# Another queue for the turned stores, loads by pair of heads, and another order of the heads

## The chip, the core and the metric

The kernel is one program on one core of a Trainium2 chip. Its metric is the device time of one execution in microseconds (us). TensorE multiplies, VectorE and ScalarE do the element-wise work, GpSimd helps, and the transfers (DMAs) are issued by SyncE (SP), ScalarE and GpSimd and carried out by 16 DMA engines. SP and ScalarE issue to a hardware queue each, GpSimd to a software queue.

## The reference

One step of an encoder layer, for a prompt of 1024 rows and for 8 sequences of 16 new rows each with 256 cached ones (the sample). Width 1024, 16 heads of 64 in four groups of four.

```
xn = rmsnorm(x, g_attn)
aq, ak, av, bq, bk, bv, cq, ck, cv, dq, dk, dv, df = split(xn @ w_in)   # w_in: 1024 x 2820
A: stick-breaking attention     w = exp(log_sigmoid(z) + later sum of -softplus(z)), causal
B: window of 128 and chunks of 64, 2 key/value heads for 4 query heads, sinks, T5 bias
C: differential attention       softmax(s1) - lam * softmax(s2), T5 bias; then rmsnorm of the head
D: forgetting attention         softmax(s + F_q - F_k), causal; F = cumsum(log_sigmoid(df + b_f))
h = x + concat(A, B, C, D) @ w_out
h = h + square(relu(rmsnorm(h) @ w_up)) @ w_down                        # 1024 x 4096
h = h + sigmoid(h @ w_ple_gate) * (p @ w_ple_proj);  y = rmsnorm(h)
```

The outputs are y, the new keys and values of each group, and the log gates. All is float32.

## The kernel before

The 1152 rows (1024 of the prompt and 128 of the sample) make nine tiles of 128, the ninth being the sample. A float32 product is made of rounded parts, a high one and a low one: `three` issues three matmuls (high x high, high x low, low x high).

**Projection.** First come the values of A and B with the gates (nine units, one for each tile), then the turned operands: queries and keys computed transposed, 128 columns of `w_in` by 384 rows a unit. `QK` lists 45 such units: for A, C and D the pieces k, q, k, q of three units each, for B k, q, q. A unit is 24 matmuls of 384 columns into one of three PSUM banks. ScalarE writes the high part (`stage_hi`, L443 or L449, and for keys a float32 copy, L448), VectorE the low part (`stage_lo`, L510, L512), and both parts are stored to scratch tensors in HBM (`q2`, `k2`: "q_turned_A" and so on). There are two staging buffers by `m % 2`: ScalarE waits for the store of unit m - 2 (`st_q`) before it writes unit m. Between the units TensorE transposes blocks of the key caches and of the new keys (`TURNS`, L638, 46 banks). A bank of the cache goes the same way: high part on ScalarE (L435), low part on VectorE (L497), into one of two `chl` buffers, stored to `kc2` ("k_cache_turned_A"); ScalarE waits for `st_c` before it overwrites one. For A, C and D each piece of keys has two banks of cache in each of its first two units. A bank of new keys goes to `krow` and from there to the key outputs. ScalarE also splits the next block's weights, one slot a unit (`split`). Last come the values of C and D (nine units) with some small work on gates and biases.

A scratch tensor holds, for each head, 64 rows (C: 32) of one half of the operand's features and then the other part's, so that a matmul over 128 partitions sums high and low. The rows are put there by this view, for all of these stores:

```python
def parts(dst, g, part):
    return dst.rearrange("(x u d) c -> u x d c", u=2, d=HALF[g])[part]
```

With a destination of 256 rows this is 2 x 64 rows for A, B and D (HALF is 64) and 4 x 32 for C. A store of a unit is 128 rows of 1536 bytes (196,608 bytes; two a unit, 90 in all: A 24, B 18, C 24, D 24). One of a cache bank is 128 rows of 2048 bytes (262,144; two a bank, 52 in all: A, C and D 16 each, B 4). GpSimd issues all of them in `qk_out` and `turned_out`, in the order of the units.

**Attention.** A loop runs twice (`heads_loop`). Each pass goes through eight jobs, two heads of each group, in the order AABBCCDD. A job is nine tiles of queries: eight of the prompt, with 128 to 1024 keys (B: up to 256), and the sample. The engines are one or two tiles apart: in step s TensorE does `scores(s + 1)`, `turn_tile(s - 1)`, `values(s - 2)`; ScalarE `evacuate_tile(s - 2)`, `exponentials(s)`; VectorE `maximum(s)`, `out(s - 3)`. VectorE prepares the next job's bias or gates at its seventh tile (`bias(nxt)`, `sample_gates(nxt)`) and waits there for all loads of that job (`job_loaded`). For a head of C, VectorE, ScalarE and GpSimd norm the outputs together in `norm`, at the tiles 5 and 6 of the next job, and GpSimd's last two operations of it (L988, L990) follow ScalarE's n_rstd.

SP issues the loads of a job when the job two before it is done (`o_full`), into one of two buffers: keys (L917), queries (L918), queries with the parts crossed (L921), the sample's cached keys (L923), its new keys (L924), its queries spread out by sequence (L925, and crossed L928), values (L929) and cached values (L930), and then what B, C or D need besides (L934 to L945; the last of B and C is L939). L924, L925 and L928 write pieces of 64 bytes. TensorE's `scores` of a job's first tile waits for all of them.

**The rest.** Output projection, MLP, input embedding and the final norm. These aren't touched.

## Time and profile before

| | |
|---|---|
| Median of 3 runs | 2264.15 us (2262.93 to 2274.48) |
| The profiled execution's own time | 2268.79 us |
| Its span, first to last instruction | 2267.2 us |
| Mean granted clock of TensorE | 0.867 |
| Busy: TensorE, VectorE, ScalarE, GpSimd | 84%, 38%, 28%, 8% of the span |
| Bytes moved by DMA | 196.88 MB, mean 87 GB/s |

The profile is of one execution. A busy share is an average over stages with different limits, so it's read by stretch. The granted clock is a share of full speed (1.00 is 2.4 GHz, 0.50 is 1.2 GHz). A DMA share is the mean busy share of the 16 DMA engines. In a list of waits the thing behind the arrow is what came last by the profile.

### The profile page before, as it was taken

Reading aid. Unit: us, or ns where it says so; the run is one execution under the profiler, and the core shown is the slowest. Engines: PE = TensorE matmul, PEld = TensorE weight load, DVE = VectorE, ACT = ScalarE, POOL = GpSimd, SP = SyncE. Lnnn points to the kernel's source line nnn. Section 1 sums busy time; section 2 is a strip of 40 time slices with the busy share of each in tenths; the row PEclk is TensorE's granted clock in tenths of the full one; section 3 lists DMA queues with packets and bytes.
Section 4 is the critical chain, followed back from the end, with each engine's and each line's share of the span. In section 5 each row is a group of like instructions: output and inputs, shape, how many; then the busy total and the mean of one; then the engine's idle time right before and its main releaser. Section 6 shows DMA issues by size and latency. Waiting matters only on the chain. (4 is left out here: it accounts for less than half of the span.)

```text
span 2267.2 us, 28303 instructions
## 1 busy us (share of the span) xinstructions
PE 1896.3 (84%) x10134; PEld 1710.8 (75%) x10134; DVE 851.6 (38%) x1619; ACT 645.1 (28%) x1387; POOL 188.0 (8%) x272
## 2 busy tenths in 40 slices
PE   6857766775848877668779999999999999999898
PEld 6857666654747776657668889899989989998686
DVE  5211222125525636535543543333333333333334
ACT  5211111014423435423332322122212212221226
POOL 0233233300000100000101000000000000000000
PEclk9978888796667776757769999999999999999999
DMA  5555565515353443544425111111211111120202
GB/s 185 143 121 135 138 149 131 105 62 126 93 130 83 127 108 88 124 116 106 109 63 176 61 56 38 38 38 38 66 47 38 38 38 38 38 65 28 76 18 98
DMA packets 257174, 196.88 MB, mean 87 GB/s; under 512 B 178044, under 2 KB 210624, under 8 KB 257016
## 3 DMA queue, kind: packets, MB, share of 16 engines
q1 hardware_dynamic: 178312, 132.75, 21.2%
q0 software_dynamic: 60032, 57.53, 10.5%
q10 hardware_dynamic: 18688, 4.72, 0.9%
q8 instruction: 88, 1.44, 0.3%
q14 instruction: 54, 0.44, 0.1%
HBM read 144.29 MB, written 54.81 MB: 88 GB/s over the span
## 5 line engine op out<-in xcount | busy, mean ns | idle before, releaser
L1346 PE MATMUL outs<-v_rows,probs_turned 128*128 128x64 f32 x984 | 166.1, 325 | 112.2 <-DVE head_out L1208 84.1
L111 PE MATMUL up<-xt_hi,w_hi_even 128*128 128x384 f32 x768 | 258.0, 336 | 1.8 <-PEq L1399 1.8
L113 PE MATMUL up<-xt_hi,w_lo_even 128*128 128x384 f32 x768 | 257.8, 336 | 0.0
L112 PE MATMUL up<-xt_lo,w_hi_even 128*128 128x384 f32 x768 | 257.6, 335 | 0.0
L1346 PEld LDWEIGHTS outs<-v_rows,probs_turned 128*128 128x128 f32 x984 | 159.0, 244 | 124.8 <-DVE head_out L1208 62.1
L113 PE MATMUL down<-w_hi_odd_b,hidden_lo 128*128 128x512 f32 x576 | 224.5, 390 | 0.0
L112 PE MATMUL down<-w_lo_odd_b,hidden_hi 128*128 128x512 f32 x576 | 224.5, 390 | 0.0
L111 PE MATMUL down<-w_hi_odd_b,hidden_hi 128*128 128x512 f32 x576 | 224.0, 389 | 0.0
L1606 DVE TENSOR_TENSOR h_rows<-down,h_rows 128x1024 f32<-128x1024 f32 x72 | 88.2, 1225 | 236.4 <-PE down L113 236.4
L1571 ACT ACTIVATE hidden_rows<-up 128x384 f32<-128x384 f32 x96 | 47.3, 492 | 417.1 <-PE up L113 417.1
L1314 PE MATMUL scores<-k_turned,q_turned_straight 128*128 128x512 f32 (+5 forms) x224 | 89.9, 519 | 69.5 <-ACT probs L1038 31.1
L111 PEld LDWEIGHTS up<-xt_hi,w_hi_even 128*128 128x128 f32 x768 | 145.0, 189 | 3.2 <-DVE xt_lo L138 2.2
L112 PEld LDWEIGHTS up<-xt_lo,w_hi_even 128*128 128x128 f32 x768 | 145.0, 189 | 0.8
L113 PEld LDWEIGHTS up<-xt_hi,w_lo_even 128*128 128x128 f32 x768 | 144.8, 189 | 0.0
L1599 DVE TENSOR_TENSOR hidden_rows<-hidden_rows 128x384 f32<-128x384 f32 x96 | 53.6, 558 | 223.8 <-ACT hidden_rows L1571 223.8
L113 PEld LDWEIGHTS down<-w_hi_odd_b,hidden_lo 128*128 128x128 f32 x576 | 108.1, 188 | 22.5
L112 PEld LDWEIGHTS down<-w_lo_odd_b,hidden_hi 128*128 128x128 f32 x576 | 108.1, 188 | 22.0
L111 PEld LDWEIGHTS down<-w_hi_odd_b,hidden_hi 128*128 128x128 f32 x576 | 108.2, 188 | 21.9
L888 ACT COPY probs_turned<-turns 128x512 f32<-128x512 f32 (+3 forms) x156 | 68.6, 459 | 148.9 <-PE turns L1333 148.5
L1333 PE MATMUL turns<-cst,probs 128*128 128x128 f32 x520 | 105.7, 333 | 1.7 <-ACT probs L1024 1.7
L1314 PEld LDWEIGHTS scores<-k_turned,q_turned_straight 128*128 128x128 f32 (+1 forms) x224 | 45.9, 260 | 80.8 <-issue 35.8
L1155 DVE TENSOR_REDUCE stats<-scores 128x1 f32<-128x272 f32 (+8 forms) x76 | 51.5, 705 | 79.0 <-PE scores L1318 78.5
(271 smaller groups left out, 3712.5 us busy)
## 6 DMA issues: line engine op xcount, KB each, us to landing
w_raw<-w_up SPq DMA_DIRECT2D x64, 256.0 KB, 2.9
w_raw<-w_down SPq DMA_DIRECT2D x64, 256.0 KB, 3.1
w_raw<-w_in SPq DMA_DIRECT2D x24, 256.0 KB, 7.6
v_rows<-value_rows SPq DMA_DIRECT2D x16, 288.0 KB, 3.7
head_rows<-head_out ACTq DMA_DIRECT2D x16, 288.0 KB, 6.4
head_rows_in<-head_rows POOLq DMA_DIRECT2D x9, 512.0 KB, 4.7
x_rows<-x_prompt SPq DMA_DIRECT2D x8, 512.0 KB, 3.7
k_cache_turned_A<-k_cache_parts POOLq DMA_DIRECT2D x16, 256.0 KB, 12.6
```

The source lines that it names most:

```text
L111: nc.tensor.matmul(out, xh, wh, start=first, stop=False)
L112: nc.tensor.matmul(out, xh, wl, start=False, stop=False)
L113: return nc.tensor.matmul(out, xl, wh, start=False, stop=last)
L888: copy(pt[i % 2][:, b * P:b * P + k], TB[n % 3][:, 0:k]).then_inc(q[f"read{n % 3}"], 1)
L1155: nc.vector.tensor_reduce(st_[:, col:col + 1], src[:, 0:n], AX.X, ALU.max, negate=True).then_inc(q["m_ready"], 1)
L1314: nc.tensor.matmul(S[UNIT[(i, m)] % 2][:, c:c + w], qt[part][own, e, P * t:P * (t + 1)], kt[own, e, k0 + c:k0 + c + w], start=part == 0, s ...
L1333: last = nc.tensor.transpose(TB[n % 3][:, (y - b) * P:(y - b + 1) * P], block_src, ident)
L1346: last = nc.tensor.matmul(dst, w[:, y * P:(y + 1) * P], vr[:, e, first_block(i) + y, :], start=y == 0, stop=y == nb - 1)
L1571: nc.scalar.activation(R[:, f % 2, :], U[f][:, 0:GT], ACT.Relu).then_inc(relu_d, 1)
L1599: nc.vector.tensor_tensor(R[:, f % 2, :], R[:, f % 2, :], R[:, f % 2, :], ALU.mult).then_inc(sq_d, 1)
L1606: nc.vector.tensor_tensor(H[:, t, :], DN[t % 2][:, :], H[:, t, :], ALU.add).then_inc(dn_add, 1)
```

## The change

The stores of turned operands and of turned cache are issued by ScalarE, to its hardware queue, in the same order and with the same views: those of unit m - 1 at the top of unit m's turn. GpSimd keeps the key rows and the values. In attention the order of the jobs is ABABCDCD, and buffers go by the job's number instead of by the head. Values are loaded once for the pair of heads of a group, in rows twice as wide, with semaphores of their own (`v_in0`, `v_in1`), for which only `values` waits. Keys and queries are loaded with the sample's columns, and GpSimd makes the sample's operands of them in `spread_operands`, three copies of 128 x 128 in the place of the DMAs L924, L925 and L928; TensorE waits for them before the sample's scores. `softplus` gets a wait for the weight buffer where a job of A follows another group.

```diff
-        def turned_out(x):
-            m, u = TURN_LIST[x]
-            if u[0] == "k":
...
-            else:
-                g, y = CACHE_LOADS[u[1]]
+        def k_rows_out(x):
+            _, u = TURN_LIST[x]
+            f = u[1]
+            if u[0] == "k" and x + 1 == k_turned(f):
+                _, g, _, pair, _, _ = QK[f * NG]
                 pool.wait_ge(c_read, x + 1)
-                dst = kc2[g][2 * P * u[2]:2 * P * u[2] + 2 * P, 512 * y:512 * y + 512]
-                n = caches_before(x) % CR
-                for part in range(2):
-                    nc.gpsimd.dma_start(parts(dst, g, part), chl[:, n, part, :].bitcast(F32)).then_inc(st_c[n], 16)
-        def qk_out(m):
-            _, g, kind, pair, _, n = QK[m]
-            pool.wait_ge(qk_lo, m + 1)
-            dst = (k2 if kind == "k" else q2)[g][2 * P * pair:2 * P * pair + 2 * P, GT * n:GT * n + GT]
-            for part, src in enumerate((stage_hi(m), stage_lo(m))):
-                nc.gpsimd.dma_start(parts(dst, g, part), src.bitcast(F32)).then_inc(st_q[m % 2], 16)
+                own = slice(P * pair, P * pair + P)
...
         for t in range(TILES):
             values_out(t, t, 0, 384)
-        x = 0
-        for m in range(len(QK)):
-            qk_out(m)
-            for _ in TURNS[m]:
-                turned_out(x)
-                x += 1
+        for x in range(NTURN):
+            k_rows_out(x)
...
+        def cache_out(x):
+            _, u = TURN_LIST[x]
+            if u[0] == "c":
+                g, y = CACHE_LOADS[u[1]]
+                act.wait_ge(c_read, x + 1)
+                dst = kc2[g][2 * P * u[2]:2 * P * u[2] + 2 * P, 512 * y:512 * y + 512]
+                n = caches_before(x) % CR
+                for part in range(2):
+                    act.dma_start(parts(dst, g, part), chl[:, n, part, :].bitcast(F32)).then_inc(st_c[n], 16)
...
+        def qk_out(m):
+            _, g, kind, pair, _, n = QK[m]
+            act.wait_ge(qk_lo, m + 1)
+            dst = (k2 if kind == "k" else q2)[g][2 * P * pair:2 * P * pair + 2 * P, GT * n:GT * n + GT]
+            for part, src in enumerate((stage_hi(m), stage_lo(m))):
+                act.dma_start(parts(dst, g, part), src.bitcast(F32)).then_inc(st_q[m % 2], 16)
...
         x = 0
         for m, (blk, g, kind, pair, col, n) in enumerate(QK):
+            if m:
+                qk_out(m - 1)
+                for y in range(x - len(TURNS[m - 1]), x):
+                    cache_out(y)
...
+        qk_out(len(QK) - 1)
+        for y in range(NTURN - len(TURNS[len(QK) - 1]), NTURN):
+            cache_out(y)
...
-vr, vc = sb("v_rows", [P, 2, TILES, HD]), sb("v_cache_rows", [P, 2, 16, HD])
...
-qt = [sb(f"q_turned_{n}", [P, 2, SEQ], F32R) for n in ("straight", "crossed")]
-kt = sb("k_turned", [P, 2, SEQ], F32R)
+vr, vc = sb("v_rows", [P, 2, TILES, P]), sb("v_cache_rows", [P, 2, 16, P])
...
+qt = [sb(f"q_turned_{n}", [P, 2, TILES * P], F32R) for n in ("straight", "crossed")]
+kt = sb("k_turned", [P, 2, TILES * P], F32R)
...
-JOBS = [(g, e) for g in GROUPS for e in range(2)]
+JOBS = [(g, e) for pair in ("AB", "CD") for e in range(2) for g in pair]
...
 def odd(i):
-    return JOBS[i // TILES][1]
+    return i // TILES % 2
+def value_buf(i):
+    return GROUPS.index(group(i)) % 2
...
-                done = q[f"job_in{e}"]
+                done = q[f"job_in{x}"]
                 half = HALF[g]
                 own = q2[g][bass.ds(P * h, P), :]
                 keys_ = k2[g][bass.ds(P * kvh, P), :]
-                crossed = [(slice(x, x + half), slice(y, y + half)) for z in range(0, P, 2 * half) for x, y in ((z, z + half), (z + half, z))]
-                def by_sequence(ap):
-                    return ap.rearrange("p (b n) -> p b n", b=DEC_B)
-                def spread(part, e):
-                    return by_sequence(qz[part][:, e, :].bitcast(F32))[:, :, 0:DEC_S]
                 sp.wait_ge(q["o_full"], at("o_full", TILES * (job - 1)))
...
-                sp.dma_start(kt[:, e, :].bitcast(F32), keys_[:, 0:SEQ]).then_inc(done, 16)
-                sp.dma_start(qt[0][:, e, :].bitcast(F32), own[:, 0:SEQ]).then_inc(done, 16)
-                for to, of in crossed:
-                    src = q2[g][bass.ds(P * h + of.start, half), :]
-                    sp.dma_start(qt[1][to, e, :].bitcast(F32), src[:, 0:SEQ]).then_inc(done, 16)
+                sp.dma_start(kt[:, x, :].bitcast(F32), keys_).then_inc(done, 16)
+                sp.dma_start(qt[0][:, x, :].bitcast(F32), own).then_inc(done, 16)
+                for y in range(0, P, 2 * half):
+                    for to, of in ((y, y + half), (y + half, y)):
+                        sp.dma_start(qt[1][to:to + half, x, :].bitcast(F32), q2[g][bass.ds(P * h + of, half), :]).then_inc(done, 16)
                 n = P * cached(g)
-                sp.dma_start(ks[:, e, :, 0:n].bitcast(F32), by_sequence(kc2[g][bass.ds(P * kvh, P), :])).then_inc(done, 16)
-                sp.dma_start(ks[:, e, :, n:n + DEC_S].bitcast(F32), by_sequence(keys_[:, SEQ:SEQ + P])).then_inc(done, 16)
-                sp.dma_start(spread(0, e), by_sequence(own[:, SEQ:SEQ + P])).then_inc(done, 16)
-                for to, of in crossed:
-                    src = q2[g][bass.ds(P * h + of.start, half), :]
-                    sp.dma_start(spread(1, e)[to], by_sequence(src[:, SEQ:SEQ + P])).then_inc(done, 16)
-                sp.dma_start(vr[:, e, :, :], vrows[:, bass.ds(V_COL[g] + HD * kvh, HD)].rearrange("(t p) d -> p t d", p=P)).then_inc(done, 16)
-                sp.dma_start(vc[:, e, 0:nb, :], cache[:, bass.ds(vcol + HD * kvh, HD)].rearrange("(s p) d -> p s d", p=P)).then_inc(done, 16)
+                sp.dma_start(ks[:, x, :, 0:n].bitcast(F32), kc2[g][bass.ds(P * kvh, P), :].rearrange("p (b n) -> p b n", b=DEC_B)).then_inc(done, 16)
+                if e == 0:
+                    v, nb = GROUPS.index(g) % 2, DEC_B * cached(g)
+                    w = HD if g == "B" else P
+                    cache = i[f"cache_{g.lower()}_kv"]
+                    vcol = 128 if g == "B" else 256
+                    sp.wait_ge(q["o_full"], at("o_full", TILES * (job_of(GROUPS[GROUPS.index(g) - 2], 1) + 1) - (0 if g in "CD" else NT)))
+                    sp.dma_start(vr[:, v, :, 0:w], vrows[:, bass.ds(V_COL[g] + w * j, w)].rearrange("(t p) d -> p t d", p=P)).then_inc(q[f"v_in{v}"], 16)
+                    sp.dma_start(vc[:, v, 0:nb, 0:w], cache[:, bass.ds(vcol + w * j, w)].rearrange("(s p) d -> p s d", p=P)).then_inc(q[f"v_in{v}"], 16)
                 if g in "BC":
                     hb = h + (4 if g == "C" else 0)
                     src = toep[bass.ds(hb, 1), 127:127 + P * (BAND - 1)].rearrange("o (p c) -> (o p) c", p=P)
-                    sp.dma_start(bi[:, e, :], src[:, 0:2 * P]).then_inc(done, 16)
+                    sp.dma_start(bi[:, x, :], src[:, 0:2 * P]).then_inc(done, 16)
                     src = toep[bass.ds(hb, 1), 127:127 + DEC_S * (BAND - 1)].rearrange("o (p c) -> (o p) c", p=DEC_S)
                     for b in range(DEC_B):
-                        sp.dma_start(bs[b * DEC_S:(b + 1) * DEC_S, e, 0:P + DEC_S], src[:, 0:P + DEC_S]).then_inc(done, 16)
+                        sp.dma_start(bs[b * DEC_S:(b + 1) * DEC_S, x, 0:P + DEC_S], src[:, 0:P + DEC_S]).then_inc(done, 16)
...
+                    sp.dma_start(fq[:, x, :], fcum_q[bass.ds(h, 1), :, :].rearrange("o p t -> (o p) t")).then_inc(done, 16)
...
+        def spread_operands(job):
+            e, n = job % 2, P * cached(JOBS[job][0])
+            job_loaded(pool, job)
+            pool.sem_inc(pool_passed, 1)
+            def by_sequence(ap):
+                return ap.rearrange("p (b n) -> p b n", b=DEC_B)
+            for part in range(2):
+                nc.gpsimd.tensor_copy(by_sequence(qz[part][:, e, :])[:, :, 0:DEC_S],
+                                      by_sequence(qt[part][:, e, SEQ:SEQ + P])).then_inc(q["spread"], 1)
+            nc.gpsimd.tensor_copy(ks[:, e, :, n:n + DEC_S], by_sequence(kt[:, e, SEQ:SEQ + P])).then_inc(q["spread"], 1)
...
             for job in range(len(JOBS)):
+                spread_operands(job)
                 spread_new(job)
                 if JOBS[job][0] == "C":
...
+            if i >= 2 and group(i - 2) != "A":
+                wait_weights_free(act, i)
             nc.scalar.activation(b, z, ACT.Abs).then_inc(q["a_abs"], 1)
...
+            if is_sample(i):
+                pe.wait_ge(q["spread"], at("spread", 3 * (job + 1)))
...
         def values(i):
-            e, nb, c = odd(i), blocks(i), cached(group(i))
+            e, nb, c = value_buf(i), blocks(i), cached(group(i))
+            own = slice(0, HD) if group(i) == "B" else slice(HD * JOBS[i // TILES][1], HD * JOBS[i // TILES][1] + HD)
             w = pt[i % 2]
             dst = OP[:, HD * (i % 2):HD * (i % 2 + 1)]
             for b in range(0, nb, 4):
                 wait_read(pe, WHERE[("tile", i, b)])
             pe.wait_ge(q["o_read"], at("o_read", i))
+            if i % TILES == 0 and JOBS[i // TILES][1] == 0:
+                pe.wait_ge(q[f"v_in{e}"], at(f"v_in{e}", 64 if group(i) in "CD" else 32))
```

Left out are the renamed indices (`job % 2` for the buffer, `JOBS[job][1]` for the head) and the counts of the semaphores.

## Rows read from the trace of the kernel before

**Rows 1.** Busy time, clock and DMA by stretch: start:end, us, each engine (instructions)

```profile
74.00:441.00 367.00, 246.15 (x1244) 237.04 (x1243) 69.02 (x123) 58.50 (x125) 116.92 (x154) 0.82 0.57 130
441.00:508.00 67.00, 55.79 (x230) 41.51 (x228) 15.04 (x27) 10.73 (x16) 6.91 (x12) 0.88 0.26 80
508.00:1190.00 682.00, 485.75 (x3096) 439.11 (x3096) 334.61 (x808) 267.46 (x656) 35.87 (x51) 0.70 0.44 106
1190.00:2267.00 1077.00, 1052.23 (x5256) 939.82 (x5256) 397.98 (x601) 272.44 (x509) 22.53 (x42) 0.98 0.17 54
```

**Rows 2.** Waits of ScalarE, 74 to 441: us in total, times, longest

```profile
ACT x_rows L443 <- DMA k_turned_A<-x_rows: 36.7, 3, 19.6
ACT k_cache_parts L435 <- DMA k_cache_turned_D<-k_cache_parts: 36.5, 4, 17.0
```

**Rows 3.** Timeline of TensorE: two matmuls with 23 between them

```profile
203.03 0.34 PE L111 MATMUL mm<-xt_hi,w_hi_even 128*128 128x384 f32 x1
...
207.19 0.34 PE L111 MATMUL mm<-xt_hi,w_hi_even 128*128 128x384 f32 x1
```

**Rows 4.** GpSimd's stores by line: L361 (turned), then L330 (values)

```profile
DMA to landing us min/median/max: 3.9/9.7/21.6
...
DMA to landing us min/median/max: 2.1/2.3/9.7
```

**Rows 5.** Busy time by stretch again; the last two columns are DMA share and GB/s

```profile
229.50:231.50 2.00, 2.00 (x14) 2.00 (x13) 0.00 (x0) 0.00 (x0) 0.43 (x1) 1.00 0.26 53
468.20:468.90 0.70, 0.70 (x4) 0.57 (x4) 0.00 (x0) 0.70 (x1) 0.00 (x0) 1.00 0.95 371
1500.00:1600.00 100.00, 100.00 (x510) 91.21 (x509) 34.59 (x50) 20.90 (x40) 0.00 (x0) 1.00 0.14 43
509.00:527.00 18.00, 1.35 (x6) 1.35 (x6) 0.00 (x0) 0.39 (x2) 0.00 (x0) 0.50 1.01 251
826.00:852.00 26.00, 24.67 (x187) 22.98 (x186) 13.29 (x29) 11.99 (x28) 0.46 (x1) 0.86 0.66 153
```

**Rows 6.** Waits of VectorE for loads, 560 to 1200: total, times, longest

```profile
DVE bias_sample L1117 <- DMA head_scalar<-rel_bias: 35.6, 3, 18.8
...
DVE head_scalar_negated L1114 <- DMA head_scalar<-swa_sinks: 28.1, 2, 14.4
DVE bias_sample L1101 <- DMA bias_sample<-fcum_sample: 21.9, 2, 11.5
```

**Rows 7.** Timeline of VectorE: start, us, what, idle before it

```profile
640.88 0.15 DVE L1114 TENSOR_SCALAR head_scalar_negated<-head_scalar 128x1 f32<-128x1 f32 x1 [13.67 <-DMA head_scalar<-swa_sinks]
```

**Rows 8.** Timeline of SP's issues, 615 to 675

```profile
619.84 0.35 SPq L917 DMA_DIRECT2D k_turned<-k_turned_B  x1
...
651.42 0.35 SPq L917 DMA_DIRECT2D k_turned<-k_turned_C  x1
...
656.16 0.70 SPq L924 DMA_DIRECT2D k_sample_turned<-k_turned_C  x1
...
665.31 0.39 SPq L929 DMA_DIRECT2D v_rows<-value_rows  x1
...
672.83 0.36 SPq L939 DMA_DIRECT2D head_scalar<-rel_bias  x1
```

**Rows 9.** Timeline of GpSimd, 725 to 800

```profile
730.54 0.45 POOL L976 TENSOR_TENSOR new_probs_by_seq<-probs,masks 128x128 f32<-128x128 f32 x1 [49.03 <-DVE probs L1180]
...
763.45 1.16 POOL L988 TENSOR_TENSOR head_out<-head_out,stats 128x576 f32<-128x576 f32 x1 [22.72 <-ACT stats L1046]
764.69 1.40 POOL L990 TENSOR_TENSOR head_out<-head_out,diff_gain_rows 128x576 f32<-128x576 f32 x1
766.03 0.69 POOL L999 DMA_DIRECT2D b_kv_sample<-value_rows  x1
```

**Rows 10.** Timeline of ScalarE and TensorE in the second head of D

```profile
838.36 1.04 ACT L1038 ACTIVATE probs<-probs,stats 128x896 f32<-128x896 f32 x1 [0.90 <-DVE stats L1155]
...
839.97 0.37 PE L1305 MATMUL scores<-k_sample_turned,q_sample_spread_straight 128*128 128x272 f32 x1
```

More of the change, by code:

```diff
@@ L726, in encoder @@
             primed_sem = sem("att_primed")
-            pe_passed = sem("pe_passed_a_wait")
+            pe_passed, pool_passed = sem("pe_passed_a_wait"), sem("pool_passed_a_wait")
             NAMES = {
                 "job_in0": "loads of the even head", "job_in1": "loads of the odd head",
-                "turned": "PE: a bank of transposes is full",
+                "turned": "PE: a bank of transposes is full", "v_in0": "loads of the values of a pair of heads of A or C",
+                "v_in1": "the same of B or D", "spread": "GpSimd: the sample's queries and new keys are spread",
                 "read0": "bank 0 is evacuated", "read1": "bank 1", "read2": "bank 2",
@@ L807, in loads, with job_of, of_bias @@
             def loads(g):
-                turned = 13 if g == "C" else 9
-                return turned + {"A": 2, "B": 12, "C": 12, "D": 4 + DEC_B}[g]
-            per = {"job_in0": 16 * sum(map(loads, GROUPS)), "turned": len(ORDER), "s_full": len(UNITS),
+                return (7 if g == "C" else 5) + {"A": 0, "B": 10, "C": 10, "D": 2 + DEC_B}[g]
+            def job_of(g, e):
+                return JOBS.index((g, e))
+            def of_bias(job):
+                return sum(g in "BC" for g, _ in JOBS[:job])
+            per = {"job_in0": 16 * sum(loads(g) for g, _ in JOBS[0::2]), "v_in0": 64, "v_in1": 64, "spread": 3 * len(JOBS), "turned": len(ORDER), "s_full": len(UNITS),
                    "b_max": 2 * TILES, "m_ready": len(UNITS) - 2 * TILES, "e_ready": len(UNITS) - 2 * TILES,
@@ L816, in encoder @@
                    "stored0": 16 * 4, "stored1": 16 * 4}
-            per["job_in1"] = per["job_in0"]
+            per["job_in1"] = 16 * sum(loads(g) for g, _ in JOBS[1::2])
             per.update({f"read{x}": len(range(x, len(ORDER), 3)) for x in range(3)})
@@ L870, in job_loaded @@
             def job_loaded(eng, job):
-                e = JOBS[job][1]
+                e = job % 2
                 eng.wait_ge(q[f"job_in{e}"], at(f"job_in{e}", 16 * sum(loads(JOBS[x][0]) for x in range(e, job + 1, 2))))
@@ L899, in body @@
                             h = 2 * j + e
+                            x = job % 2
                             kvh = j if g == "B" else h
-                            cache = i[f"cache_{g.lower()}_kv"]
-                            nb = DEC_B * cached(g)
-                            vcol = 128 if g == "B" else 256
-                            done = q[f"job_in{e}"]
+                            done = q[f"job_in{x}"]
                             half = HALF[g]
@@ L1048, in store @@
                     def store(j, job):
-                        g, e = JOBS[job]
+                        (g, e), x = JOBS[job], job % 2
                         if g == "C":
@@ L1106, in bias @@
                     def bias(job):
-                        g, e = JOBS[job]
-                        k = job - 2 + 1
+                        g, e = JOBS[job][0], job % 2
+                        k = of_bias(job) + 1
                         job_loaded(dve, job)
@@ L1343, in values @@
                         pe.wait_ge(q["o_read"], at("o_read", i))
+                        if i % TILES == 0 and JOBS[i // TILES][1] == 0:
+                            pe.wait_ge(q[f"v_in{e}"], at(f"v_in{e}", 64 if group(i) in "CD" else 32))
                         if not is_sample(i):
                             for y in range(nb):
-                                last = nc.tensor.matmul(dst, w[:, y * P:(y + 1) * P], vr[:, e, first_block(i) + y, :], start=y == 0, stop=y == nb - 1)
+                                last = nc.tensor.matmul(dst, w[:, y * P:(y + 1) * P], vr[:, e, first_block(i) + y, own], start=y == 0, stop=y == nb - 1)
                             last.then_inc(q["o_full"], 1)
```

50 lines of the change are left out of this document (22 added, 28 removed).

## The prediction

> **What bounds the kernel now.** I read the table by stretch first [rows 1]. The MLP stretch is TensorE alone, at its full clock, with 98% busy; the change doesn't touch it. The stretch of the turned operands (74 to 441 us) and attention (508 to 1190 us) hold 1049 of the 2267 us, with TensorE's granted clock at 0.82 and 0.70, which means that it idles and then runs part of its work at 1.2 instead of 2.4 GHz. Those two are what the change touches.
>
> In the first, ScalarE's waits say what ends last: it may not overwrite `stage_hi` or `chl` before earlier stores have landed [rows 2]. TensorE needs far less than the stretch takes. At the full clock one unit of 24 matmuls takes 207.19 - 203.03 = 4.16 us [rows 3], so 45 units need 187 us; with the 46 banks of transposes (my estimate: 0.5 us each) 210 us. The stretch takes 367. The stores are the bound.
>
> Why are they slow? The same GpSimd queue lands a value store of 128 plain rows (192 or 256 KB) in 2.3 us and a turned store of 192 KB in 9.7 us, medians [rows 4]. So it isn't the queue. It is the shape: `parts(...)` makes the destination 2 x 64 rows for A, B and D, and 4 x 32 for C. With two stores of B under way the core's 16 DMA engines are 26% busy, 4 engines' worth, at 53 GB/s; a plain store of the same 1536-byte rows keeps them 95% busy at 371 GB/s [rows 5]. A turned store of B runs on two DMA engines. GpSimd's queue gets its rate from several such stores side by side on different engines: 57% of 16 engines is 9 [rows 1].
>
> In attention I read VectorE's waits. It stands in `bias` and `sample_gates` for the last load of the next head, 28.1 + 35.6 + 21.9 = 85.6 us in seven waits [rows 6], in each half of the heads for B's second, C's first and D's second head. Its `out` comes behind in its order, so TensorE's `values` stops too.
>
> **Part 1, the stores go to ScalarE.** The diff keeps `parts`, so the stores stay on two DMA engines (C: four). Bytes: A, B and D make 66 stores of 196,608 and 36 of 262,144, 22.4 MB; C makes 24 and 16, 8.9 MB. What no row of before shows is on which DMA engines a run of narrow stores of a hardware queue lands. The two ends:
> - On different ones, as now: the stores run side by side and land in time. Then TensorE sets the pace, 210 us at full clock, some 240 with a clock near 0.9 and hiccups: 127 us gained.
> - All on the same two (C: four): they go one behind the other. One engine moved 371/(0.95 x 16) = 24.4 GB/s in the plain store of such rows, 43/(0.14 x 16) = 19 in the MLP, 53/(0.26 x 16) = 12.7 with narrow stores of GpSimd [rows 5]. At 24.4: 22.4/48.8 + 8.9/97.6 = 459 + 91 = 550 us; at 19: 589 + 117 = 706; at 12.7: 1057.
>
> I take the second end, at 24.4, the row of a hardware queue with the very rows of these stores. These engines also carry their sixteenth of 19 MB of loads and key rows: 1.2 MB each at 24.4, +50. In the six pieces of keys with two units of cache turns ScalarE waits for both `chl` buffers before it can issue the next stores, which leaves the engines empty for some 4 us (copies, subtraction, issues, and the start of a store; an estimate): +25. Sum 625 for 367: **+258 us**. I take this end because everything that the rows show of a narrow store is that its shape picks the number of engines, and a queue that also spreads its successive stores is a second property, seen for GpSimd's alone. ScalarE's own cost is 142 issues of about 0.4 us (SP's for a load, [rows 8]), 57 us, under its waits; VectorE's `qk_lo` is done before ScalarE asks. Behind ScalarE's waits stand `split` and the copies, which is why a late store is felt at once.
>
> On this the Trainium skill speaks against the change. Its page "DMA: Bandwidth & Descriptors", section "Why a DMA increments its semaphore by 16 and not by 1", says that the slowest dimensions of both patterns set how many engines a DMA uses, that hardware queues take always the lowest-numbered ones, and that GpSimd's takes them from a round-robin cursor. By that the sum is the +258 above. With the number of engines the trace agrees [rows 5]; which ones a hardware queue takes, no run here shows yet. The same page ("Issuing engine by pattern") calls the hardware path generally faster, which would give the other end's 240 us.
>
> **Part 2, loads of attention.** C's first head: its loads begin at 651.42, the spread DMAs take SP from 656.16 to 665.31, the last is issued at 672.83 [rows 8]. GpSimd's copies replace 9.1 us of it. VectorE reaches its wait about 5 to 7 us after the load's release (640.88 - 13.67 = 627.2, against A's end at 619.84) [rows 7, 8]. In the order ABABCDCD B1's and D1's loads have a whole job of A or C in between: those waits go. C0 still follows a short B: 12.3 us of issues + 2 to land + some 2.5 for values twice as wide, less 7.4 = 9.5 us stay; C1 follows D: about 2.5. So 85.6 - 2 x 12 = 62 us gained. The first job's loads run with the DMA engines full at 251 GB/s [rows 5]; the values and spreads leave the head of it, 4 us gained (an estimate).
>
> **Part 3, GpSimd on the path.** `spread_operands(job)` stands behind `norm` of the C head before. For D0 and D1, GpSimd can begin `norm`'s second half only after ScalarE's n_rstd, right behind exp(6), the exponentials of the tile of 896 keys: 0.6 (my estimate for two activations of nine columns) + 1.16 + 1.40, + 0.69 for a DMA (D0 only) and 3 copies at up to 0.45 (the row of a 128x128 product) [rows 9]. TensorE wants the sample's scores 0.6 us after exp(6): that ended at 839.4 and they began at 839.97 [rows 10]. Late by 5.0 us (D0) and 4.3 (D1), in a job in which TensorE is busy for 24.67 of 26 us [rows 5]: 18 us lost in four. Copies at nothing: 13; above that cover (A, B, C) they cost nothing, since GpSimd idles. ScalarE's new wait in `softplus` holds two tiles of A1 behind B's last turns, about 1 us each half: 2.
>
> Sum of attention: -62 - 4 + 18 + 2 = **-46 us**.
>
> **Sum.** 2267 + 258 - 46 = 2479 in the span. The profiled execution took 2268.8 for a span of 2267.2 and the median of the runs is 2264.15, 0.2% less; so 2475.
>
> **Rivals.**
> 1. The hardware queue spreads its narrow stores too (or uses all 16 engines). For it: 9 engines' worth is what the present queue reaches with the same shapes. Against it: only the software queue is seen doing so. 2267 - 127 - 46 = 2094, so 2090. The point where it decides: below 367 us for 31.3 MB, that is, three and a half engines busy on average at 24.4 GB/s. This is the other side.
> 2. The stores take on that queue what they take now (latency under the mix of loads stays): 2267 - 46 = 2221, so 2218. For it: the share of small transfers and loads stays.
> 3. Rival 2 without the gain of attention, because the waits for loads move elsewhere: C0's wait grows back to 19 us and the D stalls are 10: 2260. Against it: VectorE's waits name loads alone.
>
> **How the numbers follow.** Forecast 0.62; rival 1 0.24; rival 2 0.11; rival 3 0.03. The forecast's own range: 550 us without additions and 70 gained in attention gives 2380; 706 + 75 and 30 gained gives 2650. The whole range must leave out no more than 2 in 10: of rivals 1 to 3 (0.38) it has to reach down to rival 1's middle; I give 2085 to 2640. A measurement can tell 0.5% (11 us) from nothing. Faster: 0.24 + 0.11 = 0.35; same 0.03; slower 0.62.
>
> **What the profile after would show.** Step 1 right: between the two value stretches some 600 us, the share of the DMA engines near 2/16 plus the loads', landings of k_turned above 10 us on ScalarE's queue, the C part quicker than A and D. Wrong: a stretch of 240 us with TensorE's clock above 0.9. Step 2: no wait of VectorE for `head_scalar` of swa_sinks nor for `bias_sample` of fcum_sample; one of some 10 us for rel_bias. Step 3: TensorE's L1305 of D waiting 4 to 5 us for GpSimd. What would make the forecast wrong is, above all, where the hardware queue puts its stores; next the rate of one engine.

## The result, and the profile after

| | before | after |
|---|---|---|
| Median | 2264.9 us (2262.93 to 2274.48, 4 runs) | 2455.33 us (2447.79 to 2456.24, 4 runs) |
| Span of the profiled execution | 2267.2 us | 2454.7 us |
| Mean granted clock of TensorE | 0.867 | 0.843 |

The ratio is 1.0824, with a 95% interval of 1.0787 to 1.0862: 8% slower. The table by stretch of the kernel after answers to [rows 1]:

```profile
74.00:665.00 591.00, 251.43 (x1241) 240.19 (x1239) 69.67 (x123) 59.30 (x124) 8.78 (x13) 0.70 0.24 80
665.00:734.00 69.00, 56.24 (x230) 41.94 (x230) 15.04 (x28) 11.32 (x17) 6.05 (x11) 0.87 0.23 77
734.00:1367.00 633.00, 476.83 (x3096) 426.17 (x3096) 331.13 (x800) 264.64 (x649) 45.20 (x94) 0.72 0.39 109
1367.00:2454.00 1087.00, 1051.56 (x5256) 939.04 (x5256) 402.74 (x608) 276.86 (x517) 25.30 (x47) 0.98 0.17 56
```

The stretch of turned operands took 591 us for 367, and its clock fell to 0.70. SP's first load of attention stands at 733.62 for 508.08 us, 225.5 later. From there to the copy `out_turned` of the last head, at 1364.94 for 1179.41, attention took 631.3 us for 671.3, 40.0 less. What follows took 2.0 more. Sum: 225.5 - 40.0 + 2.0 = 187.5, the difference of the spans.

The list of DMA queues shows what ScalarE's queue (q10) did in the whole stretch and in those parts of it that belong to groups A, C and D, at 75 to 266, 368 to 478 and 478 to 665 us: packets, MB, and the time of its packets as a share of 16 engines.

```profile
q10 hardware_dynamic: 18099, 30.66, 14.0%
...
q10 hardware_dynamic: 4970, 8.57, 12.0%
...
q10 hardware_dynamic: 5188, 8.78, 22.2%
...
q10 hardware_dynamic: 5043, 8.67, 12.4%
```

12.0% of 16 engines is 1.92 engines: two, 96% full. In C it is 3.55 of four. In A one engine moved 8.57 MB / 191 us / 2 = 22.4 GB/s. So on average no more than two engines had work of this queue in A, though several stores were pending; stores side by side on different pairs of engines would show more. The waits of ScalarE in the stretch, which answer to [rows 2]:

```profile
ACT x_normed L449 <- issue: 224.4, 14, 26.5
ACT x_rows L444 <- issue: 57.5, 7, 10.2
ACT x_rows L444 <- DMA q_turned_B<-x_rows: 28.7, 4, 7.5
ACT k_cache_parts L416 <- DMA k_cache_turned_D<-k_cache_parts: 24.2, 4, 9.7
ACT k_cache_parts L416 <- DMA k_cache_turned_A<-k_cache_parts: 23.9, 4, 9.7
```

Most of the idle time has "issue" as its cause, and the timeline shows what that is:

```profile
208.18 0.59 ACT L416 CAST k_cache_parts<-tp 128x512 fp32r<-128x512 f32 x1 [9.66 <-DMA k_cache_turned_A<-k_cache_parts]
208.29 0.52 ACTq L432 DMA_DIRECT2D k_turned_A<-x_rows  x1
...
208.84 0.53 ACTq L432 DMA_DIRECT2D k_turned_A<-x_rows  x1
209.41 17.17 ACTq L425 DMA_DIRECT2D k_cache_turned_A<-k_cache_parts  x4
226.68 0.48 ACT L449 COPY x_normed<-mm 128x384 f32<-128x384 f32 x1 [17.49 <-issue]
```

Two stores are issued in 0.5 us each. The four behind them hold ScalarE for 17.17 us, inside the issuing instructions. The two rows of "issue" are 282 us, and that is only the idle time that ended with an issue: added up over ScalarE's timeline, the issuing instructions took about 396 of the 591 us, because an issue also stands inside many of the waits that are put down to a DMA. By line, the issues of cache stores (minimum, median, maximum in ns):

```profile
L425 ACTq DMA_DIRECT2D k_cache_turned_A<-k_cache_parts x16: 562/4904/7967, 77.3 to 221.6; - x16
L425 ACTq DMA_DIRECT2D k_cache_turned_C<-k_cache_parts x16: 547/1838/4228, 369.2 to 452.8; - x16
L425 ACTq DMA_DIRECT2D k_cache_turned_D<-k_cache_parts x16: 2504/4624/8310, 485.7 to 628.8; - x16
```

In attention, VectorE's and TensorE's waits; VectorE's row answers to [rows 6]:

```profile
DVE bias_sample L1140 <- DMA head_scalar<-rel_bias: 37.1, 4, 15.4
```

```profile
PE scores L1339 <- DMA k_sample_turned<-k_cache_turned_A: 30.1, 3, 24.7
PE scores L1330 <- POOL k_sample_turned L999: 14.7, 4, 4.2
```

The waits for `swa_sinks` and `fcum_sample` are gone. A wait of TensorE for GpSimd's spread keys is new.

### The profile page after: what moved, and what is told of

Its sections match the earlier page's. It is cut to its first block and busy times, and to the rows that moved or that the text cites. A ratio compares the mean times of both kernels' runs of the same rounds, so it can differ in the third digit from the quotient of the medians.

```text
span 2454.7 us, 28218 instructions
## 1 busy us (share of the span) xinstructions
PE 1892.4 (77%) x10134; PEld 1700.2 (69%) x10134; DVE 853.7 (35%) x1619; ACT 648.0 (26%) x1387; POOL 91.1 (4%) x178
## 5 line engine op out<-in xcount | busy, mean ns | idle before, releaser
L1374 PE MATMUL outs<-v_rows,probs_turned 128*128 128x64 f32 x984 | 154.2, 308 | 66.4 <-DVE head_out L1231 36.0
L1374 PEld LDWEIGHTS outs<-v_rows,probs_turned 128*128 128x128 f32 x984 | 146.6, 227 | 79.7 <-DVE head_out L1231 35.9
L642 PE MATMUL tp<-cst,x_normed 128*128 128x128 f32 x56 | 12.6, 348 | 241.3 <-ACT x_normed L449 239.3
L642 PEld LDWEIGHTS tp<-cst,x_normed 128*128 128x128 f32 x56 | 8.4, 176 | 244.8 <-issue 241.4
L516 DVE TENSOR_TENSOR x_rows<-mm,x_rows 128x384 fp32r<-128x384 f32 x21 | 11.7, 558 | 276.4 <-ACT x_rows L450 276.4
```

The source lines that it names most:

```text
L516: nc.vector.tensor_tensor(stage_lo(m), bank, stage_hi(m), ALU.subtract).then_inc(qk_lo, 1)
L642: last = nc.tensor.transpose(TP[x % 2][:, y * P:(y + 1) * P], src, ident)
L1374: last = nc.tensor.matmul(dst, w[:, y * P:(y + 1) * P], vr[:, e, first_block(i) + y, own], start=y == 0, stop=y == nb - 1)
```

## The experiments

In the table "stretch" runs from ScalarE's first high part of a unit of turned operands to its last, "attention" from SP's first load to the last head's `out_turned`, both in the profiled execution. "2 (4) blocks" is the shape of one store: two blocks of rows, in C four. The ratio is to the kernel before, measured beside each kernel (its median lay between 2264.9 and 2273.5), so ratios compare better than medians.

| kernel | stores | stretch | attention | median | ratio (95%) |
|---|---|---|---|---|---|
| before | GpSimd, 2 (4) blocks | 364 | 671 | 2264.9 | 1 |
| after | ScalarE, 2 (4) blocks | 589 | 631 | 2455.33 | 1.0824 |
| first | ScalarE, plain rows | 203 | 656 | 2093.15 | 0.9228 (0.9176 to 0.9279) |
| second (attention of before) | GpSimd, plain rows | 201 | 689 | 2131.14 | 0.9405 (0.9351 to 0.9459) |
| third | GpSimd, 2 (4) blocks | 361 | 632 | 2228.72 | 0.9839 (0.9786 to 0.9892) |
| fourth (attention of before) | ScalarE, 2 (4) blocks | 590 | 656 | 2495.09 | 1.1025 (1.0961 to 1.1089) |
| fifth | GpSimd, plain rows | 202 | 654 | 2098.19 | 0.9243 (0.9208 to 0.9278) |
| sixth | ScalarE, 1 block each | 279 | 632 | 2145.97 | 0.9445 (0.941 to 0.9479) |
| seventh | q, k ScalarE; cache GpSimd, 2 (4) blocks | 450 | 629 | 2313.73 | 1.0173 (1.0129 to 1.0217) |
| eighth | as sixth, two orders | 279 | 617 | 2129.14 | 0.9378 (0.9348 to 0.9407) |
| ninth | ScalarE, 4 blocks | 395 | 625 | 2262.5 | 0.9974 (0.9944 to 1.0005) |
| tenth | ScalarE, 8 blocks, two orders | 259 | 618 | 2118.15 | 0.9345 (0.9299 to 0.939) |
| eleventh | as first, two orders | 203 | 654 | 2085.15 | 0.9191 (0.9147 to 0.9236) |
| twelfth | as third, order of before | 365 | 616 | 2220.85 | 0.9802 (0.9728 to 0.9876) |

**First: the shape alone, on ScalarE's queue.** The rows of the scratch tensors are laid out so that a store is 128 plain rows, and the loads put the halves together.

```diff
-return dst.rearrange("(x u d) c -> u x d c", u=2, d=HALF[g])[part]
+return dst[P * part:P * part + P, :]
...
+straight = [(2 * half * y + half * u, half * y + P * u) for y in range(HD // half) for u in range(2)]
+for to, of in straight:
+    sp.dma_start(kt[to:to + half, x, :].bitcast(F32), k2[g][bass.ds(kb + of, half), :]).then_inc(done, 16)
```

> The changed kernel with one edit: the scratch arrays of turned operands hold a pair's high rows and then its low rows, so that each store is 128 plain rows instead of 2 blocks of 64 (C: 4 of 32); the same number of stores on ScalarE's queue, the same bytes; a head's loads come in 8 pieces (C: 16) instead of 5 (7). Theory (a store on ScalarE's queue uses as many DMA engines as its outermost dimension has entries, 2 and in C 4): the stretch of turned operands falls from 591 us to what TensorE and the evacuations need, 220 to 260, landings to 3 to 4 us, and the kernel to about 2105 (2065 to 2150). Rival (the queue itself serves one store after another at a cost of its own, or ScalarE's issues are the bound): the stretch stays above 500 and the kernel above 2360.

It took 2093.15, as expected, and the stretch 203 us, less than the 220 to 260 expected. The stretch by windows:

```profile
75.00:279.00 204.00, 202.45 (x1220) 200.21 (x1219) 68.32 (x121) 59.21 (x124) 8.47 (x12) 1.00 0.69 233
```

TensorE is busy for 202.45 of 204 us at the full clock: the stores are no bound any more. ScalarE's queue, its issues and ScalarE's waits in this kernel, a view each:

```profile
q10 hardware_dynamic: 20160, 30.94, 42.2%
```

```profile
L432 ACTq DMA_DIRECT2D q_turned_A<-x_rows x12: 338/394/877, 92.4 to 128.2; - x12
```

```profile
ACT x_rows L444 <- PE mm L113: 53.7, 17, 4.1
ACT x_normed L449 <- PE mm L113: 50.1, 17, 3.8
```

An issue takes 0.39 us (median), and ScalarE mostly waits for TensorE. The time of the packets is 0.422 x 16 x 204 = 1377 us of one engine, and in the changed kernel it was 1324 (14.0% of 16 engines in 591 us). The work of the engines is the same; only over how many it is spread has changed. The rival that the queue or the issues are the bound is out.

**Second: the same shape on GpSimd's queue, with the attention of before.** Edit as in the first.

> The kernel before with the same edit of the layout, its stores on GpSimd's queue as they were; a head's loads in 14 pieces (C: 28) instead of 9 (13). Theory (the shape bounds GpSimd's stores too): the stretch of turned operands falls from 367 us to 220 to 280 and the kernel from 2265 to 2120 to 2180. Rival (GpSimd's queue costs what it costs per store or per byte, whatever the shape): the stretch stays within 340 to 370 and the kernel within 2240 to 2275.

The kernel took 2131.14, as expected, and the stretch 201 us, less than expected. So the shape bound the kernel before too, and that rival falls. The queue of GpSimd (q0) by the two traces, first before at 74 to 441, then the second at 75 to 278:

```profile
DMA packets 64164, 47.60 MB, mean 130 GB/s; under 512 B 45255, under 2 KB 54339, under 8 KB 64149
...
q0 software_dynamic: 52341, 34.15, 45.5%
```

```profile
DMA packets 22575, 47.47 MB, mean 234 GB/s; under 512 B 3248, under 2 KB 12208, under 8 KB 22560
...
q0 software_dynamic: 10752, 34.02, 45.8%
```

The same bytes went in 52,341 packets, most under 512 bytes, and in 10,752 with plain rows. The packets' time was 0.455 x 16 x 367 = 2672 us of one engine and is 0.458 x 16 x 203 = 1488 with plain rows.

**Third and fourth: one part of the change at a time.** The third puts `qk_out` and `turned_out` back on GpSimd; the fourth moves them to ScalarE in the kernel before.

> The changed kernel with its stores of turned operands back on GpSimd's queue in the order of before: the attention part of the change alone. Theory (the two parts are independent, and the attention part gains what the two traces show between its first load and its last head, 40 us; the prediction said 46): 2225 (2215 to 2235). Rival (part of those 40 us is owed to the state that the slower stretch leaves behind, such as loads that find idle engines): 2240 to 2262.

> The kernel before with its stores of turned operands on ScalarE's queue in the order of the change: the other part alone. Theory: plus 225 us, 2490 (2480 to 2500), the stretch of turned operands near 590 us. Rival (the wide rows of the new attention loads or its later start are in that number): 2460 to 2478 or above 2510.

The third stands 39.8 us under the kernel before on its chip (2268.5), the fourth 226.6 above. Together +186.8, and the whole change measured +190.4: the parts add up. The fourth's attention, with the code of before, took 656 us for 671, so one execution's attention is known to some 15 us; the 40 rests on the medians.

**Fifth: plain rows on GpSimd's queue with the changed attention.**

> The first experiment's kernel with its stores of 128 plain rows back on GpSimd's queue. Theory (with stores that use all 16 DMA engines the queue no longer matters: the stretches of the first two experiments were 204 and 202 us, both set by TensorE): 2093 like the first, within 12 us. Rival (the hardware queue is worth something of its own once the shape is mended): 2105 or more.

2098.19, within 12 us of the first. With plain rows the two queues can't be told apart.

**Sixth: a store of one block at a time.** The layout in memory and the loads are those of the change.

```diff
-act.dma_start(parts(dst, g, part), src.bitcast(F32)).then_inc(st_q[m % 2], 16)
+half = HALF[g]
+for y in range(P // half):
+    at_ = 2 * half * y + half * part
+    act.dma_start(dst[at_:at_ + half, :], src[half * y:half * y + half, :].bitcast(F32)).then_inc(st_q[m % 2], 16)
```

> The changed kernel with its layout in memory and its loads as they are, and each store of 2 blocks of rows made 2 stores of one block of 64 rows (C: 4 stores of 32 rows) on ScalarE's queue: the same bytes to the same addresses, 364 issues in place of 142. Theory (the outermost dimension sets the number of DMA engines; the attention's 656 us in the first experiment, 25 more than in the changed kernel, come from its loads in 8 and 16 pieces): the stretch of turned operands 204 to 240 us, the attention back at 631, the kernel 2070 (2058 to 2110). Rival (it was the layout in memory or the number of issues, not the shape of one store): the stretch above 400, the kernel above 2260.

The rival is out: same addresses, and the stretch falls from 589 to 279. Attention is back at 632, which fits that the 25 us more of the first experiment are owed to its loads in pieces. But the kernel took 2146, not 2070. ScalarE's issues and what ScalarE waited for:

```profile
L251 ACTq DMA_DIRECT2D k_turned_A<-x_rows x24: 473/618/1088, 75.4 to 136.2; - x24
```

```profile
ACT x_normed L462 <- issue: 102.5, 14, 10.6
ACT x_rows L457 <- issue: 52.5, 15, 4.5
```

204 issues of 0.62 us (median; in C 160 of about 0.44) are 197 us of ScalarE's time, and 155 us of its idle time end with one. I had priced one at 0.4 us and as hidden; so many aren't.

**Seventh: q and k stores on ScalarE's queue, cache stores on GpSimd's.**

> The changed kernel with the narrow stores divided over two queues: those of queries and keys stay on ScalarE's (17.7 of 31.3 MB), those of the cache's keys go back to GpSimd's. Theory (narrow stores on the hardware queue cost their bytes over 2 or 4 engines, one after another): 12.98 MB / 48.8 GB/s + 4.72 MB / 97.6 GB/s = 314 us, times 591/550 for what the changed kernel took over its own sum of this kind, 338 (315 to 370) for the stretch and 2202 (2180 to 2235) for the kernel. Rival (each of ScalarE's issues has a price of its own as its queue is full, whatever the bytes): 90 of 142 issues remain, the stretch about 591 x 90/142 = 375 or more and the kernel 2239 or above. Rival (ScalarE's queue is held by another thing, such as the loads): above 2350.

2313.73 and a stretch of 450 us. The theory missed (315 to 370 us), and so did the rival of 2350 or above; the first rival's open bound (375 or more, 2239 or above) takes the number in, but 75 us above its own figure. In the list of waits almost none ends with an issue any more (2.8 us); the landings of both queues do, the largest of each here:

```profile
ACT x_rows L441 <- DMA k_turned_D<-x_rows: 41.9, 4, 13.6
...
ACT k_cache_parts L425 <- DMA k_cache_turned_D<-k_cache_parts: 31.7, 4, 13.5
```

That isn't because the issues went quick. They are still held, and the landing waited for comes later still: over the stretch ScalarE's timeline has about 190 us of issuing. One group of them (minimum, median, maximum in ns):

```profile
L431 ACTq DMA_DIRECT2D q_turned_A<-x_rows x12: 522/1710/5130, 117.6 to 200.2; - x12
```

```profile
q0 software_dynamic: 24320, 16.87, 18.5%
q10 hardware_dynamic: 11337, 17.08, 11.2%
```

ScalarE's queue kept 0.112 x 16 = 1.8 engines busy, of 2 (C: 4), for 17.08 MB: 21.1 GB/s per engine. The theory's sum at that rate is 307 + 56 = 363, and ScalarE waited 68 us for cache stores (31.7 + 26.6 + 9.4), in a row with its waits for the others, which makes 431. That explains most of the 450 after the fact; no run tests it, and whether the held issues are a cost of their own, as the first rival has it, stays open here. What is shown is that two queues of narrow stores that one engine waits for in turn don't add up as I supposed.

**Ninth: four blocks in every group.** With the high and low rows interleaved by 32, every store is like C's.

```diff
-return dst.rearrange("(x u d) c -> u x d c", u=2, d=HALF[g])[part]
+return dst.rearrange("(x u d) c -> u x d c", u=2, d=32)[part]
```

> The changed kernel with the high and low rows interleaved by 32 instead of 64 in A, B and D too, so that every store of turned operands is 4 blocks of 32 rows, as C's are; the same 142 stores, bytes and queue; a head of A, B or D loads its crossed operand in 4 pieces instead of 2. Theory (the number of blocks is the number of DMA engines, and the stores follow one another): 31.3 MB / 97.6 GB/s = 321 us, times 591/550 as in the changed kernel, 345 (320 to 370) for the stretch of turned operands and 2209 (2185 to 2235) for the kernel. Rival (a store with a split first dimension is slow by something else, such as ScalarE's full queue, and C was quicker by its place in the program): the stretch stays above 500, the kernel above 2360.

2262.5, a stretch of 395 us: above the theory's range (320 to 370, and 2185 to 2235 for the kernel) and far below the rival's 500. The queue and the waits say where the 50 us are:

```profile
q10 hardware_dynamic: 18364, 30.77, 21.7%
```

```profile
ACT x_normed L450 <- issue: 106.8, 12, 14.3
...
ACT k_cache_parts L417 <- DMA k_cache_turned_D<-k_cache_parts: 19.5, 4, 5.4
```

3.47 of four engines were busy on average, at 22.3 GB/s: 31.3 MB over 77 GB/s is 404. So both the rate and the fill were below what I put in. From the first to the last issue of a unit's store, A and D took 109 and 111 us, where the changed kernel has 183 and 184, and C, whose stores are the same in both, 107 for 109. So C was quicker there by its four blocks and not by its place.

**Eighth, tenth and eleventh: two changes of order in the attention**, with single blocks, with eight blocks of 16 rows and with plain rows.

```diff
-    spread_operands(job)
+    if job == 0 or JOBS[job - 1][0] != "C":
+        spread_operands(job)
     spread_new(job)
     if JOBS[job][0] == "C":
+        spread_operands(job + 1)
         norm(job)
```

In SP's `body` the block `if e == 0:` with the loads of values moves behind the loads for B, C and D.

> The kernel with single-block stores, and in the attention two changes of order: a pair's loads of values are issued behind its job's other loads, and GpSimd spreads the operands of a D job ahead of the norm of the C job. Theory (the waits read in the changed kernel's trace: VectorE for the C bias 37.1 us in 4, of which some 12 are lateness in each of the two first C jobs, and TensorE 14.7 us in 4 for GpSimd's spread keys): 25 to 40 us under the kernel with single-block stores, near 2035. Rival (what follows is late as well: the maxima and the exponentials set the pace of C and D): within 10 us of it.

> The changed kernel with high and low rows interleaved by 16 in all groups, so that every store is 8 blocks of 16 rows, and the two changes of order in the attention (loads of values last in their job, D's spread ahead of C's norm). Theory: 31.3 MB over 8 engines at 24.4 GB/s is 160 us, less than TensorE's 204 us, so that the stretch is 204 to 235; attention 631 less 17 for the two orders, plus some 5 for the crossed operand in 8 pieces; in all 2455 - 591 + 215 - 12 = 2067 (2055 to 2090). Rival (single stores are too slow on 8 engines, 3.7 us at best instead of 2.1, and ScalarE waits for them): the stretch 250 to 300, the kernel above 2100.

> The first experiment's kernel (128 plain rows on ScalarE's queue) with the same two changes of order in the attention. Theory (they gained 17 us with the single-block stores, where VectorE's wait for C's bias and TensorE's for the spread keys were 37 and 15 us; here these are 48 and 14): 2093 - 17 to 25 = 2072 (2065 to 2080). Rival (the pieces of the loads set the pace, whatever their order): 2085 or more.

The eighth is 17 us under the sixth; the theory had 25 to 40 and the rival at most 10, so neither holds. Its wait for C's bias:

```profile
DVE bias_sample L1155 <- DMA head_scalar<-rel_bias: 22.7, 4, 9.2
```

37.1 us have become 22.7, and TensorE's wait for the spread keys is no longer in the list. The eleventh took 2085.15, which misses the theory's range (2065 to 2080) and just meets the rival (2085 or more). It is 8 us under the first, but the two ran on different chips and the intervals of their ratios overlap (0.9147 to 0.9236, 0.9176 to 0.9279), so a gain from the two orders isn't shown with plain rows. It has the lowest median of the study, 0.9191 of the kernel before. The tenth took 2118 with a stretch of 259, as its rival said: its stores kept 0.357 x 16 = 5.7 of eight engines busy on average, and 66 us of ScalarE's idle time still end with an issue. Eight aren't yet enough for TensorE's 203 us.

**Twelfth: the third's kernel with the order AABBCCDD.**

```diff
-JOBS = [(g, e) for pair in ("AB", "CD") for e in range(2) for g in pair]
+JOBS = [(g, e) for g in GROUPS for e in range(2)]
```

> The third experiment's kernel (the attention part of the change alone, 2229 us) with the heads in the order AABBCCDD of before; the loads of values per pair and GpSimd's spread stay. Theory (the cheaper loads alone would have mended most of the waits: of 18.8 us of C0, 14.4 of B1 and 11.5 of D1 they take 9.1 us of issues each, and 15 where no values are loaded; and only one of two D heads still stands behind a norm): within 8 us of the third experiment's. Rival (the order is what gives a short B or D job's load a whole job of A or C to hide in): 2245 or more.

2220.85 for 2228.72, within 8 us as the theory had it, and the intervals of the two ratios overlap: no gain by the new order can be told. VectorE's waits for loads are larger than in the changed kernel:

```profile
DVE bias_sample L1136 <- DMA head_scalar<-rel_bias: 31.3, 2, 15.8
...
DVE head_scalar_negated L1133 <- DMA head_scalar<-swa_sinks: 14.0, 2, 8.1
DVE bias_sample L1120 <- DMA bias_sample<-fcum_sample: 8.1, 2, 4.2
```

```profile
PE scores L1326 <- POOL k_sample_turned L995: 6.5, 2, 3.3
```

That is 53.4 us, where the kernel before has 85.6 and the changed one 37.1. So the cheaper loads alone took away 32 of the 48.5 us, two thirds: most of them, as the theory said, but little of C0's (15.8 at most, for 18.8). The new order takes away 16 more, gives 8 back in GpSimd's (14.7 for 6.5), and its D heads are longer by more than the rest. From one `out_turned` to the next the third's D heads of the second pass took 34.6 + 30.4 us, the twelfth's 30.2 + 24.4. Why a D head behind C is longer by more than the wait for GpSimd stays open.

## Why the prediction was right

**What bounds the stretch** was right. The first experiment and the second take away only the shape, and on either queue the stretch falls to 201 to 203 us, in the first with TensorE busy for 202 of 204 us. My estimate for TensorE alone was 210. GpSimd's rate from narrow stores side by side was right too, though the nine engines of [rows 1] hold the other transfers as well: GpSimd's queue alone had 0.455 x 16 = 7.3, and at a price I hadn't seen, 1.8 times the engine time for each byte (second experiment).

**Part 1, +258, measured +226.6** by the fourth experiment (and +224 in the stretch of the two traces). Of its two ends the chosen one held: two engines 96% busy in A, 3.55 of four in C, stores one behind another. C took 109 us from its first to its last issue and D 184, so C was the quicker, as foretold. Which end it would be no row of before showed; the prediction chose between the two and gave its choice 0.62. The base, 550 us at 24.4 GB/s per engine, is in the 591; what was too large is the addition of 75, for which 41 were needed in all. By the busy shares the engines stood empty for some 8 us in A, 4 in B (1.92 of two engines in 102 us), 12 in C and 2 in D: about the 25 of the prediction. (The trace lacks the records of some 2% of the stores' bytes, so this is rough.) The term that was mis-sized is the loads' share, 50: some 16 are left for it, in the form of a slower rate, 22.4 GB/s in A. That the loads slowed it isn't shown. Its 19 MB were also too many: the stretch moved 47.6 MB before, 31.3 of them these stores, which leaves 16.3 MB and 42 us by the same rule. ScalarE's cost of 0.4 us an issue "under its waits" failed as a description, though not in the sum: once stores pile up, the issue itself holds ScalarE, for about 396 us. With engines 96% full it would otherwise have waited for the landings; that is argued, and no run takes the hold away alone.

The Trainium skill's page "DMA: Bandwidth & Descriptors", section "Why a DMA increments its semaphore by 16 and not by 1", was weighed against the change. With its number of engines the runs agree where the engines were near full: 1.92 of two in A, and 3.55 and 3.47 of four in C and in the ninth experiment. For eight and sixteen the stretches of 259 and 203 us fit, but the engines weren't full there. That a hardware queue takes the same ones each time agrees with the 1.92 engines of A; which ones they are the trace doesn't show. The same page's "Issuing engine by pattern", that the hardware path is generally faster, didn't show here: with narrow stores the stretch was 589 us on ScalarE's queue and 364 on GpSimd's, with plain rows 203 and 202.

**Part 2, -62 for the waits and -4 for the head.** (C0 and C1 are the two heads of group C in one half of the heads, and so on.) VectorE waited 37.1 us instead of 85.6 [rows 6]: 48.5 gained. B1's and D1's waits went, as said. C's didn't shrink at all, 37.1 us for 35.6, where the prediction had 24 left of them: C0 kept 15.4 us instead of 9.5, C1 4.1 and 2.2 for the 2.5 foretold. So the term for C0 was mis-sized. SP's timeline for it:

```profile
854.75 0.35 SPq L923 DMA_DIRECT2D k_turned<-k_turned_C  x1
...
855.78 3.50 SPq L927 DMA_DIRECT2D q_turned_crossed<-q_turned_C  x4
...
860.75 3.82 SPq L937 DMA_DIRECT2D v_cache_rows<-cache_c_kv  x1
864.78 4.09 SPq L941 DMA_DIRECT2D bias_prompt<-bias_rows  x1
868.96 3.62 SPq L944 DMA_DIRECT2D bias_sample<-bias_rows  x8
872.77 0.36 SPq L946 DMA_DIRECT2D head_scalar<-rel_bias  x1
```

From the first issue to the last are 18.0 us; before it was 21.4 [rows 8], and the prediction had 12.3 and 2.5 for wider values. The loads of cached values and of the bias behind them take 3.8 and 4.1 us to issue, where the first load takes 0.35. The head's wait went from 28.9 to 24.7, 4.2 gained as said. What failed here is the share given to the order. The prediction had B1's and D1's waits, 50 of its 62 us, vanish because a whole job of another head stands in between; in the twelfth, in the old order, the cheaper loads alone leave 22.1 us of them, and that kernel is no slower. So the order did at most 22 of the 50 in waits and nothing in time that can be told, and that part 2's sum came near is in part luck.

**Part 3, +18 for GpSimd, +2 for softplus.** TensorE waited 14.7 us in four places, 4.2 at most. The place was right, and the wait is gone in the eighth, where the spread stands ahead of `norm`. The prediction's 5.0 and 4.3 us don't follow from its own terms: 0.6 + 1.16 + 1.40 + 0.69 + 3 x 0.45 less 0.6 is 4.6, and 3.9 without the DMA, 17 us in four. The 2 us can't be told in the rows.

**The attention's sum, -46, measured -40** (third: -39.8; traces: -40.0). By rows it is -48.5 - 4.2 + 14.7 = -38.0. That a microsecond of wait is one of time isn't shown: the twelfth has 32 us less of VectorE's waits than the kernel before and is 47 us faster.

**The rivals.** Rival 1 (spread stores) would have shown more than two engines' worth in A. Rivals 2 and 3 need a stretch of 367, and it was 591. The 20 us between 2475 and 2455 are two errors of opposite sign, 31 too much cost in part 1 and 6 too much gain in parts 2 and 3, and some 5 that the parts measured alone leave over.

## What to carry to other kernels

Before a store changes its queue, count the entries of its outermost dimension: one narrow store uses few DMA engines on either queue, and here the hardware queue didn't make up for it with stores side by side, as GpSimd's did. Mend the shape first; the one line in `parts`, with the loads to match, brought the kernel before to 0.94 of its time (second) and the changed one from 2455 to 2093 us (first), and after it the queue made no difference. Splitting a store into many to the same end costs the issuing engine 0.4 to 0.6 us each, which is to be added up before it is called hidden.

## What the runs showed of the hardware that was not expected

- An issuing engine is held inside the issue when its hardware queue is behind: up to 8.3 us for one narrow store (17.17 for four), against 0.52 for the quickest such store and 0.39 (median) for a store of plain rows. That it is the filling of the queue is inferred from this: the time of ScalarE's issues falls with the number of engines a store uses, about 396 us of the stretch with two (C: four), 209 with four, 118 with eight and 71 with plain rows, for 142 stores each. A list of waits shows only part of it (282 us in the changed kernel, 2.8 of about 190 in the seventh). SP seems to show it as well: its load of B's keys took 4.08 us to issue behind A's cached values (4.80), and the same load of A's 0.39 (eighth experiment).
- GpSimd's queue cut the narrow stores into five times as many packets as plain ones (52,341 to 10,752 for 34 MB), and each byte cost 1.8 times the engine time (2672 to 1488 us). ScalarE's queue had 18,099 packets for 30.66 MB with narrow stores in the changed kernel and no such surcharge.
- The time of ScalarE's packets over all engines was 1324 us with 2 (C: 4) blocks, 1378 with 4, 1497 with 8 and 1377 with plain rows. With single blocks (sixth), the same bytes in 23,796 packets, it was 0.408 x 16 x 281 = 1834.
- The granted clock was 1.00 in the stretch when TensorE was busy for 202 of 204 us (first), and 0.70 when it was busy for 251 of 591 (after).
